# The second row tile of a narrow expert's down projection as fp32 products in two column halves, with the down weights loaded and split one expert later

## What is computed

```python
def step(acc, blk):                       # one block of 128 rows of one expert
    tok, g, e = blk
    xb = xpad[tok]
    hid = jax.nn.silu(xb @ w_gate[e]) * (xb @ w_up[e])    # (rows, 1024) @ (1024, 256)
    yb = (hid @ w_down[e]) * g[:, None]                   # (rows, 256) @ (256, 1024)
    return acc.at[tok].add(yb), None
```

## Time and profile before

| | |
|---|---|
| median of three runs | 2164.33 us |
| span of the profiled execution | 2167.6 us |
| TensorE matmul busy | 2061.8 us (95%) |
| VectorE busy | 1429.6 us (66%) |
| ScalarE busy | 1208.5 us (56%) |
| GpSimd busy | 572.1 us (26%) |
| DMA, mean over the span | 191 GB/s |
| the experts | about 1002 to 2100 us |

### The profile page before, as it was taken

How to read it: one execution, slowest core, us unless ns; L and a number is a source line. 1 busy time by engine, 2 the same in 40 slices (tenths; PEclk the granted TensorE clock), 3 DMA queues, 4 the chain that set the end, 5 groups by cost and what they waited for, 6 DMA issues and landing times. The chain is left out here.

```text
span 2167.6 us, 36606 instructions
## 1 busy us (share of the span) xinstructions
PE 2061.8 (95%) x11622; PEld 1747.1 (81%) x11622; DVE 1429.6 (66%) x2742; ACT 1208.5 (56%) x2133; POOL 572.1 (26%) x659
## 2 busy tenths in 40 slices
PE   8999999999999999987999999999999999999970
PEld 6778777787778888876988889889988888888860
DVE  6445444444567787877777777777777777777738
ACT  6344344343432333324777777776777777677738
POOL 2111111111012323233333333333333333333320
PEclk9999999999899999999999999999999999999995
DMA  5101101100453232346799999999999999999957
GB/s 222 55 30 37 44 30 37 44 30 27 172 194 116 79 107 87 99 170 216 230 299 278 296 288 278 301 294 278 282 295 295 291 284 289 287 286 289 286 110 302
DMA packets 113289, 413.81 MB, mean 191 GB/s; under 512 B 35184, under 2 KB 39792, under 8 KB 85520
## 3 DMA queue, kind: packets, MB, share of 16 engines
q1 hardware_dynamic: 75344, 290.02, 36.1%
q0 software_dynamic: 37872, 122.90, 25.1%
HBM read 316.91 MB, written 98.12 MB: 191 GB/s over the span
## 5 line engine op out<-in xcount | busy, mean ns | idle before, releaser
L1890 PE MATMUL ex_psU<-ex_xs,ex_guh 128*128 128x384 f32 (+5 forms) x2016 | 619.2, 371 | 0.1
L1892 PE MATMUL ex_psU<-ex_xs,ex_gul 128*128 128x192 f32 (+5 forms) x2016 | 522.4, 259 | 0.0
L1890 PEld LDWEIGHTS ex_psU<-ex_xs,ex_guh 128*128 128x128 f32 x2016 | 377.9, 187 | 31.7 <-issue 1.3
L1892 PEld LDWEIGHTS ex_psU<-ex_xs,ex_gul 128*128 128x128 f32 x2016 | 383.6, 190 | 2.5
L1650 POOL DMA_INDIRECT acc_d<-ex_y,ex_rows x128 | 197.9, 1546 | 397.1 <-ACT ex_y L1728 388.5
L1667 POOL DMA_INDIRECT ex_xg<-h_d,entries x128 | 144.0, 1125 | 344.9 <-issue 218.0
L1868 PE MATMUL ex_psY<-ex_dnh,ex_hdh 128*128 128x512 f32 x508 | 209.7, 413 | 1.7 <-DVE ex_hdl L1802 1.0
L1870 PE MATMUL ex_psY<-ex_dnh,ex_hdl 128*128 128x512 f32 x508 | 200.1, 394 | 0.0
L1869 PE MATMUL ex_psY<-ex_dnl,ex_hdh 128*128 128x512 f32 x508 | 198.9, 392 | 0.0
L1728 ACT ACTIVATE ex_y<-ex_psY,ex_use 128x512 f32<-128x512 f32 x254 | 169.4, 681 | 27.3 <-PE ex_psY L1870 26.9
L1790 DVE TENSOR_TENSOR ex_gu<-ex_psU,ex_lo 128x384 f32<-128x384 f32 (+5 forms) x128 | 77.3, 604 | 149.6 <-ACT ex_lo L1690 148.0
(11 more groups left out here) (402 smaller groups left out, 4207.0 us busy)
## 6 DMA issues: line engine op xcount, KB each, us to landing
mi_g_raw<-w_experts SPq DMA_DIRECT2D x96, 1024.0 KB
mi_g_place<-w_experts SPq DMA_DIRECT2D x96, 1024.0 KB
mi_xr<-xT SPq DMA_DIRECT2D x17, 512.0 KB, 3.6
acc_d<-de_acc SPq DMA_DIRECT2D x17, 512.0 KB, 13.3
h_d<-de_h POOLq DMA_DIRECT2D x17, 512.0 KB
de_cr<-cat SPq DMA_DIRECT2D x16, 512.0 KB
de_xr<-x_rows SPq DMA_DIRECT2D x16, 512.0 KB
mi_g_raw<-w_conv SPq DMA_DIRECT2D x6, 1024.0 KB, 16.3
```

Of the source, the lines that this page charges most:

```text
L1890: nc.tensor.matmul(psU[:, f, half, 0:2 * n].rearrange("p (s n) -> p s n", s=2), guh[:, b, kc, c0:c0 + P], rows_split(e)[:, kc, :, 0:n], st ...
L1892: last = nc.tensor.matmul(psU[:, f, half, 0:n], gul[:, b, kc, c0:c0 + P], rows_split(e)[:, kc, 0, 0:n], start=False, stop=(kc == KC - 1))
```

## The change

For experts with a cap of at most 192 (`NARROW`), 24 of them, `down` of tile 1 becomes `down_narrow`: four matmuls on plain fp32 operands, hidden values not split (`hd_full`) times the loaded weights as they are (`down_full`), in the order step 0 half 0, step 0 half 1, step 1 half 0, step 1 half 1. Column half 0 goes to PSUM partitions 0 to 63, half 1 to partitions 64 to 127 (of the other bank). So the two halves use different columns of the array. VectorE writes the columns P to n of the hidden values into `hd_full` by a multiply of its own, and the rounding and splitting of hidden values cover only the first 128 rows. For the output of half 1, whose rows lie at partitions 64 on, the gates have to stand there too: `keep_entries` becomes three copies with a drain between them.

Because the loaded down weights are now read by TensorE itself, their buffer stays in use until `down` has run. The load of the down weights is therefore issued one expert later, after the gate and up loads of the next expert, and waits for `s_dn`; rounding and splitting them move from iteration e to the same place of iteration e+1 (for all experts), counted by two semaphores of their own. In the tail the pieces 4 and 5 of expert 63 are rounded and split after the last gate_up. The two semaphores `s_passed` and `s_sp_passed` that only count waits are now shared by the stages.

The core of the diff:

```diff
+NARROW = P + P // 2
 # SyncE
-                    for kind in range(3):
-                        hold(sp, s_split, 12 * p + 6 * b - 10 + 2 * kind, s_sp_passed)
+                    for kind in range(2):
+                        hold(sp, s_split, 8 * p + 4 * b - 6 + 2 * kind, s_sp_passed)
                         w = io["w_experts"][bass.ds(e, 1), kind].rearrange("o p n -> (o p) n")
                         sp.dma_start(raw[b][:, kind], w).then_inc(s_w[b][kind], 16)
+                    if not (isinstance(p, int) and p == 1 and b == 0):
+                        load_down(2 * p + b - 1, 1 - b)
+
+            def load_down(at, b):
+                e = sp.value_load(ov[0:1, bass.ds(at, 1)], min_val=0, max_val=NE - 1)
+                hold(sp, s_dn, 4 * at - 4, s_sp_passed)
+                w = io["w_experts"][bass.ds(e, 1), 2].rearrange("o p n -> (o p) n")
+                sp.dma_start(raw[b][:, 2], w).then_inc(s_w[b][2], 16)
+            load_down(e - 1, 1)
+            hold(sp, s_dsplit, 2 * e, s_sp_passed)
 # GpSimd
+            def keep_entries(e, b, n):
+                if narrow(n):
+                    nc.gpsimd.tensor_copy(use[P // 2:P, 2 * b + 1, :], ent[0:P // 2, 2 * b + 1, :])
+                    pool.drain()
+                    nc.gpsimd.tensor_copy(use[0:P // 2, 2 * b:2 * b + 2, :], ent[0:P // 2, 2 * b:2 * b + 2, :])
+                    pool.drain()
+                    nc.gpsimd.tensor_copy(use[P // 2:P, 2 * b, :], ent[P // 2:P, 2 * b, :]).then_inc(s_use, 1)
+                else:
+                    nc.gpsimd.tensor_copy(use[:, 2 * b:2 * b + 2, :], ent[:, 2 * b:2 * b + 2, :]).then_inc(s_use, 1)
 # ScalarE, in pair
                     output(e - 2, b, (2,), n1)
-                    round_w(p, e, b, (4,))
+                    late = not (isinstance(e, int) and e == 2)
+                    if late:
+                        round_w(p if b else p - 1, e - 1, 1 - b, (4,))
                     output(e - 2, b, (3,), n1)
-                    round_w(p, e, b, (5,))
+                    if late:
+                        round_w(p if b else p - 1, e - 1, 1 - b, (5,))
 # ScalarE, tail
             copy_lo(e - 1, 1, BLK)
+            round_w(count - 1, e - 1, 1, (4, 5))
             sigmoid(e - 1, 1, BLK)
 # VectorE, activate
+                    m = split_rows(n)
                     V.tensor_tensor(gu[f][:, 0, 0:n], gu[f][:, 0, 0:n], lo[:, 0, 0:n], ALU.mult)
                     dve.drain()
-                    V.tensor_tensor(gu[f][:, 0, 0:n], gu[f][:, 0, 0:n], gu[f][:, 1, 0:n], ALU.mult).then_inc(s_hid, 1)
+                    if narrow(n):
+                        after(dve, s_dn, 4 * e - 4)
+                        V.tensor_tensor(hd_full[:, b, f, P:n], gu[f][:, 0, P:n], gu[f][:, 1, P:n], ALU.mult)
+                    V.tensor_tensor(gu[f][:, 0, 0:m], gu[f][:, 0, 0:m], gu[f][:, 1, 0:m], ALU.mult).then_inc(s_hid, 1)
 # VectorE, tail
                 sums(e - 1, f, BLK)
-                activate(e - 1, f, BLK)
+                if f == 1:
+                    split_w(e - 1, 1, (4, 5))
+                activate(e - 1, f, 1, BLK)
                 hidden(e - 1, f, 1, BLK)
 # TensorE
                 pe.wait_ge(s_hl, 2 * e + 2)
-                pe.wait_ge(s_split, 6 * e + 6)
+                pe.wait_ge(s_dsplit, 2 * e + 2)
                 r = rows_of(n, t)
+                if narrow(n) and t == 1:
+                    down_narrow(e, b, r)
+                    return
+            def down_narrow(e, b, r):
+                for f in range(FC):
+                    for half in range(2):
+                        if f == 0:
+                            after(pe, s_y, 4 * e + half + 1)
+                        at = half * (P // 2)
+                        last = nc.tensor.matmul(psY[at:at + r, half, :], hd_full[:, b, f, P:P + r],
+                                                down_full(b)[:, f, half * 512:(half + 1) * 512], start=(f == 0), stop=(f == FC - 1))
+                        if f == FC - 1:
+                            last.then_inc(s_dn, 1)
 # TensorE, tail
-            pe.wait_ge(s_split, 6 * e)
+            pe.wait_ge(s_dsplit, 2 * e)
```

More of the change, by code:

```diff
@@ L275, in step @@
                     for half, (done, sent) in enumerate(((s_u, s_wout[0]), (s_c, s_wout[1]))):
-                        hold(sp, done, TILES, s_passed)
+                        hold(sp, done, TILES, s_sp_passed)
                         sp.dma_start(w_out_raw[:, half * 4:half * 4 + 4], io["w_out"][:, half * 4:half * 4 + 4]).then_inc(sent, 16)
@@ L943, in stage_dense @@
         psU, psR = ps("psU", [P, 2 * FF]), ps("psR", [P, 512])
-        names = ("const", "passed", "sums", "zero", "cat_loaded", "x_loaded", "cat_hi", "cat_lo", "wo_attn", "wo", "wo_act", "wo_read", "var", "std",
+        names = ("const", "sums", "zero", "cat_loaded", "x_loaded", "cat_hi", "cat_lo", "wo_attn", "wo", "wo_act", "wo_read", "var", "std",
                  "h", "h_stored", "hT", "hT_hi", "hT_lo", "router", "router_copied", "logit", "score", "gu", "sig", "hid",
@@ L1545, in stage_experts @@
         sb("place_of_raw0", [P, 6 * D])
-        xs, hdh = sb("xs", [P, KC, 2, BLK], F32R), sb("hdh", [P, 2, FC, BLK], F32R)
+        xs = sb("xs", [P, KC, 2, BLK], F32R)
+        with ExitStack() as overlaid:
+            hd_full = overlaid.enter_context(nc.sbuf_tensor("ex_hd_full", [P, 2, FC, BLK], F32))
+        hdh = sb("hdh", [P, 2, FC, BLK], F32R)
         lo, gu0 = sb("lo", [P, 2, BLK]), sb("gu0", [P, 2, BLK])
@@ L1558, in stage_experts @@
         psX, psU, psY = ps("psX", [P, D]), ps("psU", [P, FC, 2, 2 * BLK]), ps("psY", [P, 2, D // 2])
-        s_const, s_passed, s_sp_passed = sem("const"), sem("passed"), sem("sp_passed")
-        s_round, s_split = sem("rounded"), sem("split")
+        s_const = sem("const")
+        s_round, s_split = sem("gate_up_rounded"), sem("gate_up_split")
+        s_dround, s_dsplit = sem("down_rounded"), sem("down_split")
         s_row = [sem(f"rows{k}") for k in range(4)]
@@ L1672, in pair @@
                     if not (early and e < 1):
-                        keep_entries(e - 1, 1 - b)
+                        keep_entries(e - 1, 1 - b, n if b else n1)
             e = 2 * pairs(pool, pair, 2)
             add_expert(e - 3, 1, BLK)
-            keep_entries(e - 1, 1)
+            keep_entries(e - 1, 1, BLK)
             add_expert(e - 2, 0, BLK)
@@ L1727, in output @@
                             after(act, s_add, 32 * (e - 1))
-                        A(y[0:r, k, half * 512:(half + 1) * 512], sums(u)[0:r], ACT.Copy,
-                          scale=use[0:r, k, 1:2].bitcast(F32)).then_inc(s_y, 1)
+                        at = slice(P // 2, P // 2 + r) if narrow(n) and u == 3 else slice(0, r)
+                        A(y[0:r, k, half * 512:(half + 1) * 512], sums(u)[at], ACT.Copy,
+                          scale=use[at, k, 1:2].bitcast(F32)).then_inc(s_y, 1)
             def first_pair(n):
@@ L1766, in pair @@
                     output(e - 2, b, (2,), n1)
-                    round_w(p, e, b, (4,))
+                    late = not (isinstance(e, int) and e == 2)
+                    if late:
+                        round_w(p if b else p - 1, e - 1, 1 - b, (4,))
                     output(e - 2, b, (3,), n1)
-                    round_w(p, e, b, (5,))
-            e = 2 * pairs(act, pair)
+                    if late:
+                        round_w(p if b else p - 1, e - 1, 1 - b, (5,))
+            count = pairs(act, pair)
+            e = 2 * count
             copy_lo(e - 1, 0, BLK)
@@ L1806, in split_w @@
                     src, hi, lo = piece(b, q)
-                    dve.wait_ge(s_round, 6 * e + q + 1)
-                    V.tensor_tensor(lo, src, hi.bitcast(F32), ALU.subtract).then_inc(s_split, 1)
+                    rounded, done, count = (s_round, s_split, 4 * e + q + 1) if q < 4 else (s_dround, s_dsplit, 2 * e + q - 3)
+                    dve.wait_ge(rounded, count)
+                    V.tensor_tensor(lo, src, hi.bitcast(F32), ALU.subtract).then_inc(done, 1)
             def split_x(p, e, t, n):
@@ L1849, in pair @@
                     hidden(e - 1, 1, 1 - b, m)
-                    split_w(e, b, (4, 5))
+                    if not (isinstance(e, int) and e == 2):
+                        split_w(e - 1, 1 - b, (4, 5))
             e = 2 * pairs(dve, pair)
```

56 lines of the change are left out of this document (29 added, 27 removed).

## The result

The changed kernel takes 2237.89 us (median of four runs, 2233.58 to 2239.62), the kernel before 2163.85 us (four runs, 2160.40 to 2165.59): a ratio of 1.0343, with an interval of 1.0331 to 1.0355. It is 74 us slower where 12.8 us faster was forecast, and it lies far outside the range of 2147.5 to 2160.5. The profiled execution of after took 2236.87 us, with a span of 2235.2.

A forecast was written before the change was run, and what follows sets the result against it. TensorE was taken to set the pace, with DMA the resource to watch. 24 x (0.73 - 0.03) = 16.8 us less and 4.0 more in the tail gave 12.8 us less, 2151.5 us, range 2147.5 to 2160.5.

The forecast's parts named there:

- the paragraph on GpSimd: `keep_entries` on GpSimd: three copies and two drains take 1.3 us; an extra 1.5 us and 0.7 fit the slack, cost 0.
- If the cover goes, only the adds come later: GpSimd's queue behind `keep_entries`: without slack only the adds are late, and their buffers have a whole iteration; cost 0.
- Rival C: Experts: late split rows or DMA become a second limit, leaving half the gain, 0.35 us each; 2159.9 us, chance 13%.
- The block: `down` of tile 1 on TensorE: 2.79 us replaced by 2.06 us, a gain of 0.73 us per expert.
- A: `down_narrow`: column halves do not overlap, block about 3.7 plus 0.2 us; 30 us slower, 2195 us, chance 5%.
- B: `down_narrow`: halves overlap in part under strict order, block 2.5 us, gain 0.29 us each; 2161.3 us, chance 7%.
- The waits on the other engines: Around `down` and gate_up: `output` wait 0.03 us, split rows ready with 0.2 to 0.3 us to spare, later units cost 0.
- the wait of 0.03 us: Start of `down_narrow`: TensorE waits 0 to 0.1 us for unit 1 of `output`, taken as 0.03 us per expert.
- DMA: Narrow experts: bytes stay, 15.7 us busy against a 15.66 us period at cap 192; counted 0, 3 us kept for the range.
- The tail: After the last gate_up: step 1 of `down` starts 3.2 us later, 0.8 us for a slower clock; +4.0 us, bounds +3.2 to +8.
- "Cost 0" for the moved down weights: Load, rounding and splitting one expert later: no engine gets more work, the load has a 15.6 us period; no path cost.
- the sum's own range: Total time from 0.62 to 0.76 us gain per expert and a tail of 3.2 to 8 us: 2149.5 to 2157.4 us.

The follow-up runs named there:

- drain_alone: The kernel before with one drain ahead of the single copy of `keep_entries` in the 24 narrow experts: 2216.80 us, ratio 1.0249.
- one_column_half: The changed kernel with a plain single copy in `keep_entries` and all four calls on PSUM partitions 0 on: 2196.96 us (one run).
- half_by_half: gate_by_vector with both steps of half 0 ahead of those of half 1: 2159.15 us (one run).
- gate_by_vector: The changed kernel with `keep_entries` back to one copy without drains, VectorE moving the gates to partitions 64 on: 2154.95 us, ratio 0.9963.
- move_only: The changed kernel with `NARROW = 0`: no narrow block, no drains, down weights still one expert later, tail changed: 2174.32 us, ratio 1.0055.
- early_last_load: gate_by_vector with expert 63's last down-weight roundings and splits ahead of the last copy and sums, and their load issued earlier: 2146.03 us, ratio 0.9927.
- one_drain_less: The changed kernel without the second of the two drains, the three copies kept: 2235.73 us, ratio 1.0341.

## Why the prediction was wrong

**The step that failed** is in the paragraph on GpSimd: "three copies and two drains are bounded by 0.4 and 2.5 us, and I take 1.3", and behind it "Cost 0". The drain was priced like the copies around it, by what it does itself, and not by what is outstanding when it runs. Just ahead of the copy at 1202.08 in the earlier trace rows the second of two indirect adds is issued, which those rows leave out:

```profile
1201.15 1.40 POOL L1650 DMA_INDIRECT acc_d<-ex_y,ex_rows  x1 [3.04 <-ACT ex_y L1728]
```

The first drain of after waited 7.8 to 11.3 us, until such adds had landed. The bound was no bound: none of the rows of before shows a drain on GpSimd, and none excludes one of 10 us. "If the cover goes, only the adds come later" failed too. Behind `keep_entries` on the same engine stand the gathers, SyncE's load of the entries waits for it, and the next adds stand behind the gathers. So the ring closes on GpSimd and SyncE alone, without TensorE: drain, entries (about 3 us), gathers, adds, drain, some 18 to 19 us against a period of 15.2 to 15.7. That TensorE has no part in it is read from the adds: from the first drain to the last, in after and in `drain_alone`, GpSimd is never idle for more than 1.13 us before one, while in the kernel before it waited 2.85 and 3.04 us for ScalarE's outputs. The mean turn (23 turns each, between starts) shows what gave way, as first add to second add + second add to last copy + last copy to gather + gather to gather + gather to next add: before 4.4 + 0.9 + 5.5 + 1.5 + 3.8 = 16.1 us, `drain_alone` 2.1 + 8.3 + 3.8 + 1.6 + 2.8 = 18.6 us. The drain costs 7.4 us, and the ring had 4.9 us to give. The prediction had the queue in view but checked its slack only against 1.5 us. `drain_alone` shows the loss by itself, with 53.6 us.

**Rival C** had the mechanism's shape, a second limit on the experts, and named GpSimd only among the signs. Its price, half the gain, left out that a second limit can lie above the old period and then takes all the gain and more.

**The block.** Forecast 0.73 us of gain for each; measured 0.7 to 0.73 by the periods, with 1.86 from first start to gate_up and about 0.1 us more at the first step of gate_up (0.27 instead of 0.16). The calls of `values` carry over to 48 columns, to another bank for the second half and to a wait between the first calls. A is refuted; `one_column_half` shows what it would have cost (forecast 3.7, measured 3.56 us per block). B, which asked for blocks of 2.5 us, is refuted by the same 1.86 us, and `half_by_half` shows that not even the program order matters.
The Trainium skill (TensorE: Matmul & The Clock Gate, Part 3: Packing small matmuls) says that matmuls start and end in strict order. The 1.86 us in both program orders disagree with that for calls of different column halves, and the measurement decides.

**The waits on the other engines** were right: `gate_by_vector` shows no idle time of TensorE among the experts up to the tail, and the wait of 0.03 us isn't seen (15.2 against 15.24). VectorE's new multiply takes 0.21 to 0.23 us (taken: 0.15, in bounds of 0.1 to 0.3). DMA was right as well, if closely: a share of 0.98 and no wait.

**The tail** was forecast at +4.0 us (3.2 to 8) and costs 10.8 us in the trace of `move_only` (11.1 by the medians); this is the second step that failed, though it is the smaller. The part that the prediction described was sized within its bounds: in `gate_by_vector`, from the last half of gate_up to the last matmul it takes 17.6 us instead of 12.2, +5.4, the clock's share included (some 10 matmuls at half the clock, 2 us, where 0.8 was taken). The other part, +6.2 us (from the start of the last first half of gate_up to the last half, 18.3 instead of 12.15), was missing: the last down load now lies across the end of the loop, where TensorE branches out. The stall is 3.3 us longer than before, and behind it 13 matmuls come 0.43 us apart, at half the clock, instead of 0.23. "Cost 0" for the moved down weights held for all experts but the last. The step looked at who waits for the load, not at what the load stands in the way of.

**With the two steps mended** the sum comes out: 24 x 0.73 = 17.5 us less, and a tail as before, against 15.6 measured for `early_last_load`. The rest, 1.9 us, is under half of the 0.2% that a measurement can tell. (The lower end of the sum's own range should read 2149.3 instead of 2149.5: 24 x 0.76 - 3.2 = 15.0. It changes nothing.)

## What to carry to other kernels

Price a drain on GpSimd by what the engine has outstanding, not by what it orders: behind indirect adds it lasted here until the data had landed. If one lies in a ring of engines, add up the whole ring, with the waits in it that can give way, and compare it with the period before calling it hidden. The small copy that has to change partitions cost nothing measurable on VectorE, where it needed no drain. When a transfer is moved, look at the last turn of the loop by itself, at what is awaited there and at what the transfer overlaps.

## What the runs showed of the hardware

- A drain on GpSimd behind two indirect adds lasts until 0.20 to 0.46 us after their last landing (72 drains in after, `drain_alone` and `one_drain_less`); a second one, with a copy between, takes 0.25 to 1.2 us (24 in after).
- TensorE's branch out of the loop of pairs takes 3.4 to 3.7 us (three kernels), and 6.0 to 7.3 us with the 1 MB load in flight (seven kernels). In all ten it ends 2.4 to 2.5 us behind the start of a 16 KB packet of code, and this packet starts 0.9 to 1.3 us into the branch in the three and 3.6 to 4.9 us in the seven.
- Plain fp32 calls of 512 columns on one column half start 0.86 to 0.91 us apart (3.56 us for four); alternating halves, four take 1.86 us, whichever half the program names first.
- In the tails TensorE's matmuls were 0.43 us apart (half the clock), for 6 to 13 matmuls, behind every idle time of 3.4 to 4.6 us (at times only from the fifth matmul on), and 0.23 us apart behind those of 0.71 to 0.99 us.
